# Second block's attention: a masked key tile left out, mask and maximum in one instruction, one norm for all heads, rotation sums on VectorE

## The reference

```python
h = rms_norm(x, pre_mix_g[l])
proj = h @ w_in[l]
qa, ka, va, qb, kb, vb, gates = jnp.split(proj, split_at, axis=-1)
qa, ka = apply_rope(qa, cos_a, sin_a), apply_rope(ka, cos_a, sin_a)
oa = diff_attention(qa, ka, va, lam)      # 4 heads, causal, (softmax1 - lam*softmax2) @ v
oa = rms_norm(oa, diff_head_g[l]) * (1.0 - lam_init)     # over each head's 128 features
ya = oa.reshape(b, s, A_WIDTH) @ w_a_out[l]
qb, kb = apply_rope(qb, cos_b, sin_b), apply_rope(kb, cos_b, sin_b)
# 4 heads x 3 groups: causal windows (128,1), (512,4), (2048,16), merged by log-sum-exp
yb = ob.reshape(b, s, B_WIDTH) @ w_b_out[l]
mix = (sigmoid(g_a) * ya + sigmoid(g_b) * yb) @ w_mix_out[l]
# then the residual, and a feed-forward network with a causal convolution
```

## Time and profile before

| | |
|---|---|
| Median of 3 runs | 1649.29 us (1648.39 to 1651.22) |
| Profiled execution: its own time, its span | 1651.56 us, 1649.8 us |
| TensorE matmul busy | 1521.5 us, 92% |
| TensorE weight loads: busy; mean of one, group L457 | 1279.0 us, 78%; 195 ns |
| VectorE busy | 953.0 us, 58% |
| ScalarE busy | 684.6 us, 41% |
| GpSimd busy | 106.8 us, 6% |
| Mean granted TensorE clock | 0.952 |
| Weight chunk, issue to landing, 214 issues | 4.8 us |
| Stage of the change: first projection chunk, first product of B, first product behind B | 1134.7, 1312.5, 1387.3 us |

### The profile page before, as it was taken

The page is one execution under the profiler, slowest core; times in us unless marked ns, Lnnn a source line. Parts: engine busy times, 40 slices in busy tenths (PEclk is TensorE's granted clock), DMA queues, the critical chain, the costliest instruction groups (busy, mean ns, idle before and its releaser), DMA issues.

```text
span 1649.8 us, 23391 instructions
## 1 busy us (share of the span) xinstructions
PE 1521.5 (92%) x9340; PEld 1279.0 (78%) x9340; DVE 953.0 (58%) x1311; ACT 684.6 (41%) x1064; POOL 106.8 (6%) x111
## 2 busy tenths in 40 slices
PE   5999899889999999989887899997988899799997
PEld 3786366668887888879745788997888899698986
DVE  2577553563232424577736555567887665576866
ACT  3421344454131413463234644455334464464544
POOL 1300000000000000028000000000122000000000
PEclk7999889889999999989999899998989999999999
DMA  9422166122221404154254354444533433434543
GB/s 389 137 82 97 70 234 251 59 103 102 82 96 51 153 25 153 51 173 166 102 215 194 130 201 163 166 181 154 179 106 133 145 108 139 162 130 179 186 183 114
DMA packets 34336, 236.94 MB, mean 144 GB/s; under 512 B 4304, under 2 KB 4432, under 8 KB 6736
## 3 DMA queue, kind: packets, MB, share of 16 engines
q1 hardware_dynamic: 31936, 228.29, 37.6%
q0 software_dynamic: 2320, 7.51, 1.7%
HBM read 234.73 MB, written 2.00 MB: 143 GB/s over the span
## 4 chain that ended last, share of the span: by engine, by line
PE 78%; DVE 12%; ACT 5%; DMA 3%; issue 2%; SPq 0%; DVEq 0%; ACTq 0%
PE ps L457 41%; PE ps L495 22%; PE ps L473 4%; PE ps L558 2%; DVE w_lo L370 2%; DMA w<-in_stream 2%; PE ps L671 2%; DVE tiny L1632 1%; PE ps L704 1%; DMA C<-in_consts 1%; ACT w_hi L360 1%; PE ps L563 1%; PE ps L676 1%; ACT U L1175 1%; DVE U L1584 1%
## 5 line engine op out<-in xcount | busy, mean ns | idle before, releaser
L457 PE MATMUL ps<-h_hi,w_hi 128*128 128x256 f32 (+1 forms) x1600 | 509.3, 318 | 6.0 <-DVE h_lo L1436 4.6
L457 PE MATMUL ps<-h_lo,w_hi 128*128 128x256 f32 (+1 forms) x1600 | 505.2, 316 | 0.0
L457 PE MATMUL ps<-h_hi,w_lo 128*128 128x256 f32 (+1 forms) x1600 | 504.6, 315 | 0.0
L370 DVE TENSOR_TENSOR w_lo<-w,w_hi 128x1024 fp32r<-128x1024 f32 x332 | 403.1, 1258 | 79.3 <-ACT w_hi L360 77.6
L360 ACT ACTIVATE w_hi<-w 128x1024 fp32r<-128x1024 f32 x332 | 331.4, 1053 | 229.7 <-DMA w<-in_stream 229.4
L457 PEld LDWEIGHTS ps<-h_hi,w_hi 128*128 128x128 f32 x1600 | 312.1, 195 | 28.1 <-issue 7.8
L457 PEld LDWEIGHTS ps<-h_lo,w_hi 128*128 128x128 f32 x1600 | 312.1, 195 | 17.2
L457 PEld LDWEIGHTS ps<-h_hi,w_lo 128*128 128x128 f32 x1600 | 311.5, 195 | 17.3
L495 PE MATMUL ps<-w_hi,g_hi 128*128 128x512 f32 x472 | 188.7, 400 | 3.7 <-DVE g_lo L1892 3.5
L495 PE MATMUL ps<-w_hi,g_lo 128*128 128x512 f32 x472 | 187.8, 398 | 0.0
L495 PE MATMUL ps<-w_lo,g_hi 128*128 128x512 f32 x472 | 187.6, 398 | 0.0
(11 more groups left out here) (242 smaller groups left out, 1770.0 us busy)
## 6 DMA issues: line engine op xcount, KB each, us to landing
w<-in_stream SPq DMA_DIRECT2D x214, 1024.0 KB, 4.8
U<-rpb_rows POOLq DMA_DIRECT2D x32, 64.0 KB, 2.4
SW<-in_small POOLq DMA_DIRECT2D x2, 896.0 KB, 7.2
X<-in_x SPq DMA_DIRECT2D x1, 1024.0 KB, 13.0
X<-in_ctx SPq DMA_DIRECT2D x1, 1024.0 KB, 15.1
X<-in_masks POOLq DMA_DIRECT2D x1, 1024.0 KB, 5.0
GA<-in_gpost POOLq DMA_DIRECT2D x2, 512.0 KB, 5.0
out<-X SPq DMA_DIRECT2D x2, 512.0 KB, 2.6
```

Source lines behind the costliest of these rows:

```text
L370: dve.tensor_tensor(k.w_lo[:, c.slot, half], k.w[:, c.slot, half], k.w_hi[:, c.slot, half].bitcast(f32), ALU.subtract).then_inc(k.lo_done, 1)
L457: last = pe.matmul(k.banks(2 * c.pair, n, j * (512 if tiles == 2 else n)), w[a][:, c.slot, at:at + 128], h[b][:, kt * stride:kt * stride + n],
```

## The change

- The first 128 queries no longer meet the second 128 keys: scores, masks, exponentials, transposes and values leave that tile out, in A and in B. `A_WIDTH` is 384 columns for two query tiles, `B_WIDTHS` 384 and 768.
- Mask, scale and maximum become one instruction, `tensor_tensor_reduce`, per query tile (and per softmax in A): it adds the mask, multiplies by the negative scale and takes the minimum. Each comes with a second instruction that reads its accumulator. The exponential then works with scale -1.
- A's output is made with tokens on the partitions. ScalarE squares it with a running sum and copies it; one root, one reciprocal and one product serve all four heads behind chunk 22; eight transposes bring the result back to features, beside the first gate chunk.
- VectorE adds the rotation's two parts (L1802 now), and GpSimd's 16 sums go.
- In the projections both splits now run a chunk further ahead and stand elsewhere: ScalarE's for j+3 stands behind the copy and ahead of the exponentials, VectorE's behind `rotated` and `probs_a` and ahead of the maxima. Chunk 23 has none.

```diff
--- before.py
+++ after.py
@@ -177,8 +177,19 @@
 def head_steps(j):
 
     n = j - HEAD_A
-    return [(head, step) for step, at in (("norm", 4), ("scores", 0), ("transposes", 2), ("values", 3))
+    return [(head, step) for step, at in (("scores", 0), ("transposes", 2), ("values", 3))
             for head in range(HEADS) if n == 4 * head + at]
+
+
+def causal(qt):
+
+    return 128 * qt, 128 + 128 * qt
+
+
+A_WIDTH = 384
+B_WIDTHS = (384, 768)
+OA_SUMS, OA_RSTD = 112, 120
...
@@ -758,37 +769,46 @@
...
-            for cmp in range(2):
-                rows = slice(64 * cmp, 64 * cmp + 64)
-                for qt in range(2):
-                    last = pe.matmul(k.banks(4, 256, (cmp * 2 + qt) * 256),
+            for qt in range(2):
+                at, width = causal(qt)
+                for cmp in range(2):
+                    rows = slice(64 * cmp, 64 * cmp + 64)
+                    last = pe.matmul(k.banks(4 + cmp, width, at),
                                      b["qa"][rows, hd * 256 + qt * 128:hd * 256 + qt * 128 + 128],
-                                     b["ka"][rows, hd * 256:hd * 256 + 256], start=True, stop=True)
+                                     b["ka"][rows, hd * 256:hd * 256 + width], start=True, stop=True)
...
-            for kt in range(2):
-                for qt in range(2):
-                    at = (hd % 2) * 1024 + qt * 256 + kt * 128
-                    last = pe.transpose(k.banks(6, 128, kt * 256 + qt * 128), b["pa"][:, at:at + 128], ident)
+            for block in range(3):
+                at = (hd % 2) * 2 * A_WIDTH + block * 128
+                last = pe.transpose(k.banks(6, 128, block * 128), b["pa"][:, at:at + 128], ident)
...
-            for kt in range(2):
-                last = pe.matmul(k.banks(7, 256), b["va"][:, kt * 512 + hd * 128:kt * 512 + hd * 128 + 128],
-                                 b["pta"][:, (hd % 2) * 512 + kt * 256:(hd % 2) * 512 + kt * 256 + 256],
-                                 start=kt == 0, stop=kt == 1)
+            for block, (qt, kt) in enumerate(((0, 0), (1, 0), (1, 1))):
+                pt = (hd % 2) * A_WIDTH + block * 128
+                last = pe.matmul(k.banks(7, 128, qt * 128), b["pta"][:, pt:pt + 128],
+                                 b["va"][:, kt * 512 + hd * 128:kt * 512 + hd * 128 + 128],
+                                 start=kt == 0, stop=kt == qt)
...
+    def heads_a(two):
+
+        if two:
+            pe.wait_ge(k.s("oa_lo"), 1)
         else:
-            pe.wait_ge(k.s("oa_sq"), hd + 1)
-            pe.matmul(k.banks(7, 256, 256), ones, b["oa_sq"], start=True, stop=True).then_inc(k.s("oa_ssq"), 1)
+            pe.wait_ge(k.s("oa_n"), 1)
+        for n in range(4):
+            at = two * 512 + n * 128
+            last = pe.transpose(k.banks(7, 128, n * 128), b["oa"][:, at:at + 128], ident)
+        last.then_inc(k.s("oa_t"), 1)
...
@@ -817,10 +838,13 @@
...
+        if hd == 0:
+            pe.wait_ge(k.s("oa_lo"), 2)
         for n in range(6):
             grp, kt = n // 2, n % 2
-            at = kt * 1536 + (grp * 4 + hd) * 128
-            last = pe.matmul(k.banks(7, 256), b["vb"][:, at:at + 128], b["ptb"][:, n * 256:n * 256 + 256],
+            at, width = kt * 1536 + (grp * 4 + hd) * 128, 256 - 128 * kt
+            pt = grp * 384 + kt * 256
+            last = pe.matmul(k.banks(7, width, kt * 128), b["vb"][:, at:at + 128], b["ptb"][:, pt:pt + width],
                              start=n == 0, stop=n == 5)
...
@@ -830,17 +854,17 @@
...
-    pe.wait_ge(k.s("oa"), HEADS)
+    heads_a(0)
     scores_b(0)
     for hd in range(HEADS):
         gate(2 * hd)
+        if hd == 0:
+            heads_a(1)
         pe.wait_ge(k.s("p_b"), hd + 1)
         for grp in range(3):
-            for kt in range(2):
-                for qt in range(2):
-                    at = qt * 768 + grp * 256 + kt * 128
-                    last = pe.transpose(k.banks(4, 128, (grp * 2 + kt) * 256 + qt * 128), b["pb"][:, at:at + 128],
-                                        ident)
+            for qt, kt in ((0, 0), (1, 0), (1, 1)):
+                at = grp * 128 if qt == 0 else 384 + grp * 256 + kt * 128
+                last = pe.transpose(k.banks(4, 128, grp * 384 + (qt + kt) * 128), b["pb"][:, at:at + 128], ident)
...
@@ -1246,47 +1270,59 @@
...
-            if hd:
-                act.wait_ge(k.s("oa"), hd)
-            act.activation(b["oa_sq"], k.banks(7, 256), ACT.Square).then_inc(k.s("oa_sq"), 1)
-        else:
-            act.wait_ge(k.s("oa_ssq"), hd + 1)
-            act.activation(b["oa_std"], k.banks(7, 256, 256), ACT.Sqrt, bias=eps,
-                           scale=1.0 / 128).then_inc(k.s("oa_std"), 1)
+            for qt in range(2):
+                at = OA_SUMS + 2 * hd + qt
+                o.then(act.activation(b["oa_sq"][:, qt * 128:qt * 128 + 128], k.banks(7, 128, qt * 128), ACT.Square,
+                                      accum_out=k.tiny[:, at:at + 1]))
+            act.activation(b["oa"][:, hd * 256:hd * 256 + 256], k.banks(7, 256), ACT.Copy).then_inc(k.s("oa"), 1)
+            if hd == HEADS - 1:
+                o.wait()
+                act.activation(k.tiny[:, OA_RSTD:OA_RSTD + 8], k.tiny[:, OA_SUMS:OA_SUMS + 8], ACT.Sqrt, bias=eps,
+                               scale=1.0 / 128).then_inc(k.s("oa_std"), 1)
...
     act.wait_ge(k.s("lam_exp"), 1)
+    feed_hi(k, act, At(c0 + 2))
     for j in range(24):
         c = At(c0 + j)
-        feed_hi(k, act, c + 2)
         kind = KINDS[c.first]
         if kind in ("va", "vb"):
             at = (j - 4) * 256 if kind == "va" else (j - 18) * 256
             act_take(k, act, c, b[kind][:, at:at + 256], 256, 0).then_inc(k.act_read, 1)
+        if j < 23:
+            feed_hi(k, act, c + 3)
         for hd, step in head_steps(j):
             step_a(hd, step)
...
@@ -1746,8 +1785,6 @@
...
-        if turned >= 2:
-            dve.wait_ge(k.s("rope2"), turned - 1)
...
@@ -1755,87 +1792,100 @@
...
-            dve.tensor_tensor(two(m), k.two(c, 256, src),
-                              sin[src].unsqueeze(1).broadcast_to([wide, 2, 256]), ALU.mult)
-        dve.tensor_tensor(two(b[kind][:, at:at + 512]), k.two(c, 256),
-                          cos.unsqueeze(1).broadcast_to([128, 2, 256]), ALU.mult).then_inc(k.dve_read, 1)
+            o.then(dve.tensor_tensor(two(m), k.two(c, 256, src),
+                                     sin[src].unsqueeze(1).broadcast_to([wide, 2, 256]), ALU.mult))
+        to = b[kind][:, at:at + 512]
+        dve.tensor_tensor(two(to), k.two(c, 256), cos.unsqueeze(1).broadcast_to([128, 2, 256]),
+                          ALU.mult).then_inc(k.dve_read, 1)
+        o.wait()
+        dve.wait_ge(k.dve_read, DVE_READ_COUNT[c.first])
+        dve.tensor_tensor(to, to, b["swapped"][:, (turned % 2) * 512:(turned % 2) * 512 + 512],
+                          ALU.add).then_inc(k.s("rope2"), 1)
...
     def chunk(j):
         c = At(c0 + j)
-        feed_lo(k, dve, c + 2)
         if KINDS[c.first] in ("va", "vb"):
             values(c, j)
         else:
             rotated(c, j)
-        for hd, step in head_steps(j):
-            step_a(hd, step)
-
         if j > HEAD_A and (j - HEAD_A) % 4 == 1 and (j - HEAD_A) // 4 < HEADS:
             probs_a((j - HEAD_A) // 4)
+        if j < 23:
+            feed_lo(k, dve, c + 3)
+        for hd, step in head_steps(j):
+            if step == "scores":
+                maxima_a(hd)
...
-        sc = k.banks(4, 1024).rearrange("p (c n) -> p c n", c=2)
-        o.link(dve.tensor_tensor(sc, sc, b["mask_a"].unsqueeze(1).broadcast_to([128, 2, 512]), ALU.add))
-        nm = k.tiny[:, 32 + 4 * (hd % 2):36 + 4 * (hd % 2)]
-        o.link(dve.tensor_reduce(nm, k.banks(4, 1024).rearrange("p (m n) -> p m n", m=4), AX.X, ALU.max,
-                                 negate=True))
-        dve.tensor_scalar(k.tiny[:, 40 + 4 * (hd % 2):44 + 4 * (hd % 2)], nm, 0.125, None,
-                          ALU.mult).then_inc(k.s("nmax_a"), 1)
+        for cmp in range(2):
+            for qt in range(2):
+                (at, width), m = causal(qt), 40 + 4 * (hd % 2) + 2 * cmp + qt
+                sc = k.banks(4 + cmp, width, at)
+                last = dve.tensor_tensor_reduce(sc, sc, b["mask_a"][:, at:at + width], -0.125, HUGE, ALU.add, ALU.min,
+                                                k.tiny[:, m:m + 1])
+        last.then_inc(k.s("nmax_a"), 1)
...
-            dve.wait_ge(k.s("oa_std"), hd + 1)
-            o.link(dve.reciprocal(b["oa_std"], b["oa_std"]))
-            o.link(dve.scalar_tensor_tensor(b["oa_f"], k.banks(7, 256), k.tiny[:, 70:71], b["oa_std"],
-                                            ALU.mult, ALU.mult))
-            at = 2048 + hd * 256
-            o.link(dve.tensor_copy(k.h_hi[:, at:at + 256], b["oa_f"]))
-            dve.tensor_tensor(k.h_lo[:, at:at + 256], b["oa_f"], k.h_hi[:, at:at + 256].bitcast(f32),
-                              ALU.subtract).then_inc(k.s("oa"), 1)
-
+    feed_lo(k, dve, At(c0 + 2))
```

(42 more changed lines are left out.)

68 lines of the change are left out of this document (40 added, 28 removed).

## The result

| | before | after |
|---|---|---|
| median of the runs, us | 1649.0 (1648.0 to 1651.2, 6 runs) | 1614.2 (1611.0 to 1616.5, 6 runs) |
| profiled execution (span), us | 1651.6 (1649.8) | 1614.2 (1612.4) |
| first projection chunk to first product behind attention B, us | 252.6 | 217.5 |
| of it, from the first head's scores on, us | 208.4 | 174.3 |

The account below looks back on a forecast made before the run. The prediction took the stage to be bound by VectorE's queue order, TensorE waiting once in four chunks. Its terms, 14.7 + 6.0 + 0.7 + 9.3 + 1.3 + 1.4 = 33.4 us, took 1649.3 to 1615.9 us, range 1609 to 1627.

Parts of the forecast that it names:

- Waits of L775: In attention A, TensorE's transposes wait four times for VectorE's probabilities; all 14.7 us were to go.
- the slow clock: TensorE's slower chunks and transposes around the attention A waits; 6.0 us were to go with those waits.
- The margin: In attention A, the first head's probabilities were to be ready 0.6 us before TensorE wants them.
- a second cause: VectorE's lateness in the projections: weight splits take 3.44 us beside GpSimd's sum and 2.35 us without it.
- The first four chunks: Sums moved to VectorE in the first projection chunks; a 0.9 us TensorE wait shrinks to about 0.2, 0.7 won.
- TensorE's own work: Fewer columns in attention A (4.0 us) and B (6.2), less 0.9 for eight new transposes; net 9.3 us won.
- The turn and B's head 0: From attention A to B, a 1.8 us wait falls to 0.5, 1.3 won; B's first head loses its 1.4 wait.
- A rest of the waits: Rival: attention A's probabilities stay 0.65 to 1.75 us late at each head; 1621 to 1625 us, chance 0.20.
- Narrow products don't pay: Rival: weight loads set the pace of TensorE's 128-column products, so 8.6 of 9.3 us go; 1624.5 us, chance 0.08.
- Another cause: Rival: exponentials or hops between engines alone made attention A's four waits, which stay; 1636.6 us, chance 0.05.
- The fused instruction as the bound: Rival: VectorE's fused mask and maximum runs at 5.6 ns an element and costs 32 us; 1648 us, chance 0.04.

Follow-up runs that it names:

- e1: The kernel before with only the new order of the ScalarE and VectorE queues; 1636.9 us, ratio 0.9913 to the kernel before.
- e6: The changed kernel with two idle reciprocals on VectorE ahead of each attention A head's maxima, +1.7 us a head; 1618.4 us, ratio 0.9800 to the kernel before.
- e7: The changed kernel with four idle reciprocals on VectorE ahead of each attention A head's maxima, +3.3 us a head; 1623.6 us, ratio 0.9837 to the kernel before.
- e3: The changed kernel with the rotation sums back on GpSimd; 1616.3 us, ratio 0.9796 to the kernel before.
- e4: The changed kernel with mask, maximum and scale as separate instructions again; 1616.5 us, ratio 0.9792 to the kernel before.
- e9: The changed kernel with both the rotation sums on GpSimd and mask, maximum and scale unfused; 1615.5 us, ratio 0.9807 to the kernel before.
- e5: The changed kernel with TensorE's removed columns given back as products and transposes nothing needs; 1625.3 us, ratio 0.9864 to the kernel before.
- e2: The changed kernel with the old order of the queues; 1622.2 us, ratio 0.9820 to the kernel before.

## Why the prediction was right, step by step

- *Waits of L775, 14.7, and the slow clock, 6.0.* Right in sum: no L786 wait, and from the second projection chunk on clock 1.00 and every chunk 5.75 or 5.76. From the first scores to B's first scores 133.6 us became 107.1; of these 26.4 the prediction had 25.6. e1 shows that the order alone would have left 7.4 us of waiting and two slow chunks (6.65), so order and relief of VectorE were both needed, and the prediction was right to count on both for this one term.
- *The margin.* 0.91 us by the order of time and 1.0 by e6 and e7, for a predicted 0.6. The maxima took 1.36 us, the lower bound, and not 2.1, because the accumulator reads lie beside the next instruction. Of the 0.74 us won by that, 0.33 didn't reach the margin: VectorE then stood until chunk 7 was done.
- *What made the margin.* Here the prediction weighed the parts wrongly. It called GpSimd's sums a second cause and worried about the fused instruction; neither edit alone moves the gauge (e3, e4), and both together cost 1.7 us (e9). VectorE's busy time in four chunks fell by 5.9 us from e1 to the changed kernel (28.9 to 23.0). Of that the sums make 1.6 (24.6 in e3), the fusing 0.8 (23.8 in e4), and the head's norm about 3.0 by its rows in e1 (1206.94 to 1209.91). So the norm, which the prediction left out of VectorE's sum without a price, was the largest part of the relief. What it is worth in time stays an estimate, as it was not put back: e7 adds 3.3 us at its place and costs 9.6, but ahead of the first head too, where no norm stood; only two of its three waits have a norm's place.
- *The first four chunks.* 0.7 forecast. From the start of the second chunk to that of the seventh TensorE took 30.32 us before and 29.69 after, 0.6 less, so the size was about right. It was placed wrongly: the wait shrank from 0.90 to 0.66 and not to 0.2, and the rest lay at the chunk ahead, whose wait of 0.2 is gone. In e3, with the sums on GpSimd, the waits are 0.9 and 0.2 again, so its cause is shown. The small one, before and in e3:

```profile
PE ps L473 <- issue: 0.2, 1, 0.2
```

```profile
PE ps L484 <- issue: 0.2, 1, 0.2
```

- *TensorE's own work, 9.3 net.* Right: 10.36 by e5 for the columns, 10.2 forecast, from which 0.9 for the transposes of A's heads goes (0.46 ahead of B's scores and 0.44 in B).
- *The turn and B's head 0.* 0.6 left for a predicted 0.5, and nothing of 1.4. From B's first scores on 74.8 us became 67.2; of these 7.6 the prediction had 7.2.
- *What the sum left out.* The two parts won 1.2 us more than forecast. Five waits went whole, and a wait costs about 0.2 us more than its row (last section), which makes an estimate of 1.0. The first projection chunk took 0.45 us less than before (8.06, 7.61), which was luck: in the eleven other executions it took 7.48 to 8.43.
- *The rivals.* A rest of the waits: none. Narrow products don't pay: 12 records take 1.97 for 1.96 forecast. Another cause: e1 and e2 show the order's share. The fused instruction as the bound: it takes 0.29 to 0.47 us in A, and at most 1.00 us, for 768 columns, in B.
